# Conditioning rows of a DiT-style block turned into columns by on-chip copies from GpSimd's queue, with six rows' weights read with a stride

## The reference

```python
    silu_c = jax.nn.silu(c)
    silu_cc = jax.nn.silu(c_ctx)[None]
    for l in range(DEPTH):                       # DEPTH = 2
        mod = silu_c @ w_ada[l] + b_ada[l]
        mod_c = silu_cc @ w_ada[l] + b_ada[l]
        sh1, sc1, g1, sh2, sc2, g2 = jnp.split(mod, 6, axis=-1)
        csh1, csc1, cg1, csh2, csc2, cg2 = jnp.split(mod_c, 6, axis=-1)
        h = modulate(rms_norm(x, norm1_g[l]), sh1, sc1)
...
        x = x + g1[:, None, :] * y
        h = modulate(rms_norm(x, norm2_g[l]), sh2, sc2)
        x = x + g2[:, None, :] * expert_choice_ffn(h, ...)
```

## Time and profile before

| | us |
|---|---|
| median of 3 runs | 2315.06 (2312.73 to 2321.35) |
| span of the profiled execution | 2316.9 |
| TensorE busy | 2036.9 (88%) |
| VectorE busy | 670.7 (29%) |
| ScalarE busy | 430.6 (19%) |
| GpSimd busy | 0.2 |
| matmuls of `mod_step`, L1252, 18 pieces | 71.1 |
| turns at L1265, four pieces | 8.3 |
| turns at L1268, eight pieces | 16.4 |
| first block's attentions | about 150 to 270 and 1151 to 1221 |

### The profile page before, as it was taken

The page is one execution under the profiler, slowest core; times in us unless marked ns, Lnnn a source line. Parts: engine busy times, 40 slices in busy tenths (PEclk is TensorE's granted clock), DMA queues, the critical chain, the costliest instruction groups (busy, mean ns, idle before and its releaser), DMA issues.

```text
span 2316.9 us, 21565 instructions
## 1 busy us (share of the span) xinstructions
PE 2036.9 (88%) x8606; PEld 1003.2 (43%) x8606; DVE 670.7 (29%) x1613; ACT 430.6 (19%) x884; POOL 0.2 (0%) x4
## 2 busy tenths in 40 slices
PE   6999899999988889888999978789776688979998
PEld 3445444444432323333554433333222255748863
DVE  2275311124211212124560132122211158730001
ACT  3045300014200000002151022103100032530000
POOL 0000000000000000000000000000000000000000
PEclk8999999999999989998999988999897899989999
DMA  9237722322599999996394548999999963132432
GB/s 366 76 145 304 270 82 64 101 90 109 216 421 422 430 428 429 429 427 243 127 345 137 191 199 330 425 420 422 431 427 429 429 237 109 37 109 102 153 136 82
DMA packets 111614, 598.15 MB, mean 258 GB/s; under 512 B 9255, under 2 KB 15223, under 8 KB 86811
## 3 DMA queue, kind: packets, MB, share of 16 engines
q1 hardware_dynamic: 107920, 591.82, 63.9%
q10 hardware_dynamic: 3595, 4.95, 0.6%
HBM read 595.71 MB, written 1.05 MB: 258 GB/s over the span
## 4 chain that ended last, share of the span: by engine, by line
PE 70%; DMA 21%; DVE 4%; ACT 2%; issue 2%; DVEq 0%; SPq 0%; ACTq 0%
PE bank L1286 24%; DMA weight_ring<-in_w_up_e 14%; PE bank L1696 8%; PE bank L638 7%; PE bank L1723 4%; PE bank L1679 4%; PE bank L657 3%; PE bank L1235 3%; PE bank L1252 3%; DMA weight_ring<-in_w_down_e 2%; DMA arena<-in_w_up_e 2%; PE bank L1522 2%; PE bank L435 2%; PE bank L1456 2%; DMA weight_ring<-in_w_ada 1%
## 5 line engine op out<-in xcount | busy, mean ns | idle before, releaser
L1286 PE MATMUL bank<-weight_ring,arena 128*128 128x512 f32 (+1 forms) x1328 | 562.0, 585 | 4.0 <-DMA weight_ring<-in_w_in 2.0
L1286 PEld LDWEIGHTS bank<-weight_ring,arena 128*128 128x128 f32 x1328 | 252.7, 191 | 308.8 <-issue 299.1
L1696 PE MATMUL bank<-weight_ring,arena 128*64 128x512 f32 x832 | 247.1, 642 | 55.3 <-DMA weight_ring<-in_w_up_e 43.2
L1679 PE MATMUL bank<-weight_ring,arena 128*32 128x512 f32 x816 | 152.5, 767 | 67.4 <-DMA weight_ring<-in_w_up_e 52.7
L1723 PE MATMUL bank<-weight_ring,arena 128*64 128x512 f32 (+1 forms) x800 | 179.1, 593 | 12.3 <-DMA weight_ring<-in_w_down_e 11.2
L1696 PEld LDWEIGHTS bank<-weight_ring,arena 128*64 128x64 f32 x832 | 80.0, 148 | 180.0 <-issue 179.7
L638 PE MATMUL bank<-arena,weight_ring 128*128 128x256 f32 x704 | 153.6, 381 | 0.8 <-DVE small L2339 0.8
L3100 ACT ACTIVATE arena<-bank 64x512 f32<-64x512 f32 (+1 forms) x64 | 37.7, 589 | 624.6 <-PE bank L1696 398.1
L638 PEld LDWEIGHTS bank<-arena,weight_ring 128*128 128x128 f32 x704 | 134.7, 191 | 19.7 <-issue 1.1
L1235 PE MATMUL bank<-const,arena 128*128 128x128 f32 (+3 forms) x764 | 106.1, 286 | 33.8 <-DVE arena L2504 6.4
L1235 PEld LDWEIGHTS bank<-const,arena 128*128 128x128 f32 (+3 forms) x764 | 90.5, 165 | 84.6 <-issue 64.2
(11 more groups left out here) (388 smaller groups left out, 1840.8 us busy)
## 6 DMA issues: line engine op xcount, KB each, us to landing
weight_ring<-in_w_up_e SPq DMA_DIRECT2D x52, 2048.0 KB, 14.3
weight_ring<-in_w_gate_e SPq DMA_DIRECT2D x51, 2048.0 KB, 16.1
weight_ring<-in_w_down_e SPq DMA_DIRECT2D x50, 2048.0 KB, 13.1
weight_ring<-in_w_in SPq DMA_DIRECT2D x25, 2048.0 KB, 10.0
weight_ring<-in_w_ada SPq DMA_DIRECT2D x24, 2048.0 KB, 12.3
arena<-in_w_down_e SPq DMA_DIRECT2D x14, 2048.0 KB, 15.8
arena<-in_w_gate_e SPq DMA_DIRECT2D x13, 2048.0 KB, 16.4
arena<-in_w_up_e SPq DMA_DIRECT2D x12, 2048.0 KB, 17.3
```

The source lines that it names most:

```text
L1286: mm = pe.matmul(b[:, 0:c1 - c0], lhs[:, k, t * P:t * P + P], slot_view(r)[:, k, c0:c1], start=(k == 0), stop=(k == ks - 1))
L1679: mm = pe.matmul(b[c:c + R, :], xgT[1][:, KH * half + k, e, :], wide(r)[:, k, n * 512:n * 512 + 512], start=(half == 0 and k == 0), stop=( ...
L1696: mm = pe.matmul(banks_[n][c:c + R, :], xgT[l][:, KH * half + k, e, 0:R], wide(r)[:, k, n * 512:n * 512 + 512], start=(half == 0 and k == ...
```

## The change

Only `mod_step` inside the attentions changes (`late=True`); the two early pieces are multiplied and turned as before.

- TensorE no longer turns the ten late rows. The matmuls of L1265 are gone altogether, those of L1268 stay for the two early pieces.
- GpSimd gets a stream: for each of the ten rows it waits until the row is in `row_tmp` and issues four DMAs (two streams, two halves of the row), each from one partition to 64 partitions, 8 consecutive numbers for each, into a new tile `mod_turned`.
- VectorE waits on the semaphore of these DMAs (`row_turned0` or `row_turned1`, 64 for four DMAs) in place of a full bank, at the same place, and reads `mod_turned` in place of the bank.
- A copy can only give partition p eight numbers that lie side by side. For the four pieces that want element 8p+k that is right as it is. For the six others, `(1, 0)`, `(1, 1)`, `(2, 0)`, `(2, 1)`, `(2, 3)`, `(2, 4)`, the row itself has to be made in another order: their matmuls at L1252 (L1257 after) read the weights with the inner step of 128 numbers (512 bytes), 8 of them, then the next column. The number of matmuls and of columns stays.

```diff
+        mod_turned = sb("mod_turned", 2, 2, KD)
...
-            def mod_step(cur, turned):
+            def mod_step(cur, turned, late=True):
                 if cur:
                     l, seg = cur
+                    by_partition = late and seg % 3 != 2 and not (l < DEPTH and seg > 2)
...
-                                mm = pe.matmul(b[at:at + 32, :], silu_pad[:, col:col + 32], wide(r)[:, k, n * 512:n * 512 + 512],
+                                row = wide(r)[:, k, n * 512:n * 512 + 512]
+                                if by_partition:
+                                    row = wide(r)[:, k, :].rearrange("q (k p) -> q p k", p=P)[:, 64 * n:64 * n + 64, :]
+                                mm = pe.matmul(b[at:at + 32, :], silu_pad[:, col:col + 32], row,
                                                start=(k == 0), stop=(k == KH - 1))
...
-                if turned:
+                if turned and not late:
                     pe.wait_ge(S("seg_row_ready"), due("seg_row_ready"))
                     pe.wait_ge(S("freeD"), due("freeD"))
                     b = bank_of("D", T.n["freeD"])
...
-                            if turned[0] < DEPTH and turned[1] > 2:
-                                mm = pe.matmul(b[64 * n:64 * n + 64, 2 * k:2 * k + 2], row_tmp[q, k:512:KD], ident[q, pair], start=True, stop=True)
...
+        @block.gpsimd
+        def _(pool):
+            rows_ready = 2
+            for l in range(DEPTH):
+                for _, turned in LATE_STEPS[l].values():
+                    if turned:
+                        rows_ready += 1
+                        at = turned[1] % 3
+                        pool.wait_ge(S("seg_row_ready"), rows_ready)
+                        for n in range(2):
+                            for s in range(2):
+                                q = 64 * at + 32 * n + s
+                                pool.dma_start(mod_turned[64 * n:64 * n + 64, at, s, :],
+                                               row_tmp[q:q + 1, :].rearrange("o (p k) -> o p k", k=KD)).then_inc(S(f"row_turned{at}"), 16)
...
+                    if late:
+                        dve.wait_ge(S(f"row_turned{seg % 3}"), due(f"row_turned{seg % 3}", 4 * 16))
+                        dve.tensor_tensor(col, mod_turned[:, seg % 3, :, :].rearrange("p s k -> p k s"), bias, ALU.add).then_inc(S("dve_step"), 1)
+                        dve.wait_ge(S("dve_step"), due("dve_step"))
```

More of the change, by code:

```diff
@@ L1263, in mod_step @@
                             q, pair = slice(base, base + 34), slice(base + 32 * n, base + 32 * n + 2)
-                            if turned[0] < DEPTH and turned[1] > 2:
-                                mm = pe.matmul(b[64 * n:64 * n + 64, 2 * k:2 * k + 2], row_tmp[q, k:512:KD], ident[q, pair], start=True, stop=True)
-                            elif k // KH == n:
+                            if k // KH == n:
                                 at = (k % KH) * P
@@ L1893, in _ @@
             pe.wait_ge(S("silu_c_ready"), due("silu_c_ready", 2))
-            mod_step(*EARLY_STEPS[0])
+            mod_step(*EARLY_STEPS[0], late=False)
             pe.wait_ge(S("vecs_landed"), 16 * (N_VEC - N_VEC0))
@@ L1899, in _ @@
             mm.then_inc(S("fullD"), 1)
-            mod_step(*EARLY_STEPS[1])
+            mod_step(*EARLY_STEPS[1], late=False)
             turn_half(xn, 0, "A", 1)
             pe.wait_ge(S("silu_c_ready"), due("silu_c_ready", 4))
-            mod_step(*EARLY_STEPS[2])
+            mod_step(*EARLY_STEPS[2], late=False)
             turn_half(xn, 1, "A", 1)
-            mod_step(*EARLY_STEPS[3])
+            mod_step(*EARLY_STEPS[3], late=False)
             pe.wait_ge(S("router_pad_clear"), 1)
@@ L2053, in mod_step @@
                     l, seg = turned
-                    dve.wait_ge(S("fullD"), due("fullD"))
-                    b = bank_of("D", T.n["fullD"])
                     col = mod_cols[:, 2 * l + seg // 3, 1 - seg % 3, :, :]
@@ L2058, in mod_step @@
                     bias = (vec_rows[:, l, seg - 2, :] if by_row else vecs[:, l, 32 + 8 * seg:40 + 8 * seg]).unsqueeze(2).to_broadcast([P, KD, 2])
-                    dve.tensor_tensor(col, b[:, 0:16].rearrange("p (k s) -> p k s", s=2), bias, ALU.add).then_inc(S("freeD"), 1)
-                    dve.wait_ge(S("freeD"), due("freeD"))
+                    if late:
+                        dve.wait_ge(S(f"row_turned{seg % 3}"), due(f"row_turned{seg % 3}", 4 * 16))
+                        dve.tensor_tensor(col, mod_turned[:, seg % 3, :, :].rearrange("p s k -> p k s"), bias, ALU.add).then_inc(S("dve_step"), 1)
+                        dve.wait_ge(S("dve_step"), due("dve_step"))
+                    else:
+                        dve.wait_ge(S("fullD"), due("fullD"))
+                        b = bank_of("D", T.n["fullD"])
+                        dve.tensor_tensor(col, b[:, 0:16].rearrange("p (k s) -> p k s", s=2), bias, ALU.add).then_inc(S("freeD"), 1)
+                        dve.wait_ge(S("freeD"), due("freeD"))
                     if seg % 3 == 1:
@@ L2698, in _ @@
             for step in EARLY_STEPS[1:]:
-                mod_step(*step)
+                mod_step(*step, late=False)
             dve.memset(flag, 0.0).then_inc(S("mod_cols_ready"), 1)
```

## The result

| | before | after |
|---|---|---|
| median of 20 runs, us | 2316.60 | 2323.91 |
| ratio to before, 95% interval | | 1.0034 (1.0023 to 1.0044) |
| span of the profiled execution, us | 2316.9 | 2317.5 |
| layer 0's attention, from piece `(0, 3)` to the router sums | 106.8 | 102.7 |
| layer 1's attention, from piece `(2, 0)` to the router sums | 63.8 | 73.3 |

The change makes the kernel slower by about 7.9 us, 0.34%: a small loss, inside the half per cent that I called no change that can be told, though twenty runs a side do tell it. The two attentions move against each other: layer 0's gets shorter by 4 us, layer 1's longer by 9.5.

The account below looks back on a forecast made before the run. TensorE, busy 88%, bounds the kernel, except where layer 0's attention waits for weights. Removed turns, clock and copies sum to -16.0 us, strided reads +19.9: +3.9 on 2315.1, so 2319 us, range 2296 to 2362.

Parts of the forecast that it names:

- What bounds where: Both attentions: TensorE full in layer 1, a turn costing 1.88 us; in layer 0 weights late from about 214 us.
- the stretch that waits for weights: Layer 0's attention, from the end of piece (1, 0)'s matmuls to (1, 5) at 257.58; removing turns there gains 0.
- Turns removed and the clock: Ten late turns gone: -4.0 and -2.0 us in layer 0, -7.5 in layer 1; clock -3.1; copies +0.7; about -16.
- The 3.1 us for the clock: Layer 0, behind the turns of (0, 3) and (0, 4): TensorE's slowdown goes with them; bounds 0 and 3.1 us.
- Copies: GpSimd's 40 DMAs, 256 packets a row: landing after 8.1 us costs 0; their DMA traffic adds 0.7 us.
- the 2.0 us that the prediction gives beside it: Fixed time for a small DMA issued by GpSimd, from the Trainium skill; the sum would stay as it is.
- Rival 3: Copies land late and VectorE waits in place of TensorE: 17 us at a 13.7 us landing, 2316 us; chance 0.06.
- The stride: Six pieces' matmuls read weights 512 bytes apart; taken as a factor of 2 on the matmuls, price 19.9 us.
- d: Time by which one strided piece becomes longer than a packed one; taken as 3.57 us, bounds 0 and 10.7.
- 6d - 1.5: Price of six longer strided pieces, less 1.5 us that (1, 1) may be late without cost; 19.9 us.
- Rival 1: The strided reads of the six pieces cost nothing: -16.0 us, 2299 us, or 2296.5 with a calmer clock; chance 0.22.
- rival 2: Four strips share the read at L1257, a strided bundle taking up to four times as long: +46.7, 2362 us; chance 0.27.

Follow-up runs that it names:

- experiment 2: Against the changed kernel, all weights read packed, GpSimd still copying all ten rows (six pieces' columns in another order): 2303.59 us, ratio 0.9944 to the kernel before.
- experiment 1: Against the changed kernel, TensorE turns all ten rows again and GpSimd copies nothing; strided weight reads stay: 2345.25 us, ratio 1.0124 to the kernel before.
- experiment 6: Against the changed kernel, a late piece's matmuls reordered so the four column strips run one after another, same output: 2429.68 us in one run.

## Why the prediction was right

Forecast 2319 us, +3.9 us, from a range of 2296 to 2362; measured +7.9 us by the ratio. The mechanism that I took for the likeliest is the one that was there: the turns' gain is taken back by the strided reads. That the time fell inside a range of 66 us says little; the forecast's own, 2312 to 2327, holds it too. Of the 4.9 us between 2319 and 2323.9, 1.5 are the base, three runs against twenty. By its steps:

- **What bounds where.** Held in the main. Turns in the stretch that waits for weights turned into waiting (with the copies alone 10.0 us for 5.3). Those of layer 1 were worth their length in the changed kernel and 4.9 of 7.5 us without the stride. What I left out is that TensorE's clock falls behind these waits, so that longer waits cost something beside the load.
- **Turns removed and the clock**, -16.0 with the copies' cost: measured in experiment 2 as -13.0 (-16.9 to -9.0). Too large in layer 1: I gave the weights of `(2, 5)` 1.6 us to spare, and in experiment 2 TensorE waited 1.79 us for them and 0.70 for VectorE at `(2, 4)`. The four pieces were in 46.6 us after the end of `(2, 0)` there (1194.20 less 1147.62), where I had summed 42.4. The 3.1 us for the clock were seen to be gone in the profile, and both profiles of the kernel before had them; by experiment 1 they are no fixed part of the turn.
- **Copies.** Cost 0 held, VectorE waited 0.3 us. I took the landing as 8.1 us from a row of another queue, and it was 5.1 (4.8 at least, 6.4 at most); the 2.0 us that the prediction gives beside it was not seen either. The packets were half as many as counted. Rival 3 never came near.
- **The stride.** The term that was mis-sized: d = 3.57 us by a factor of 2, measured 4.43 by 2.24. The price 6d - 1.5 becomes 25.1 us, and the sum -16.0 + 25.1 = +9.1, within the measured 5.3 to 10.2. The waits of experiment 2 do not lower it, as with the strided pieces they are not there. The row that led to the factor had about the right size: the strided weight loads of the earlier trace rows, 1.66 against 0.67 ns a column, and not the turns of the earlier trace rows. That the two kinds of read are slow for one reason no run shows, so the size of the factor is in part luck.
- **Rivals.** Rival 1 (free stride) falls by the 8.00 us; rival 2 by experiment 6; rival 3 by the waits.
- **By attention.** Layer 1's was to become longer by 4 x 3.57 - 7.5 = 6.8 us and became 9.5 longer. Its four strided pieces cost 17.9 us more and the turns 7.5 less, and 0.9 of `(2, 0)` is covered: behind it TensorE waited 0.59 us for ScalarE between two groups of turns of the probabilities, and now they run through. I had let all of d through there. Layer 0's was to lose 2.8 (8.4 of gains less 5.7 of stride) and lost 4.1 and 5.7 in the two pairs of profiles. Up to the start of `(1, 0)` it lost 9.0 and 7.7 us, where I had 7.1; from there on it became 4.8 and 2.0 longer, where the sum with d = 4.43 gives 6.1. The rest lies in the spread between profiles, of which the clock behind the waits is a part, and is not assigned.

## What to carry to other kernels

A moving fp32 operand whose neighbours lie 16 bytes or more apart cost TensorE twice its matmul time and a little more (512 columns, 32-wide stationary operand; the turns of the earlier trace rows, 16 in 1.94 us with a stride of 8, did not pay it); put a reordering where an engine with time to spare reads the data anyway, here into VectorE's emptying of the bank, where it cost nothing. Work taken off TensorE is only worth what is on the path in that stretch: 7.5 us of turns gave 4.9 where the weights were near to being late, and nothing clear where they were late already. Small on-chip copies issued by an idle GpSimd are a good way to turn rows into columns when one step of some 9 us lies between making and using them.

## What the runs showed of the hardware that I had not expected

- Two numbers out of each 16 bytes, neighbours or 8 bytes apart, are enough for nearly full pace (3.80 us for a piece read in pairs against 3.64 packed, some 5% more), one is half pace or a little less (7.3 to 8.7 us), with little regard to the step, from 16 to 512 bytes.
- VectorE reads a PSUM bank at a step of 512 bytes as fast as packed: 683 ns for 34x512 in both cases.
- Four column strips side by side are 2.5 times as fast as one after another (3.57 against 8.79 us), not four times.
- Behind waits of 2.8 to 3.7 us for weights a packed piece took 5.0 to 6.6 us in place of 3.64, at a granted clock of 0.54 to 0.72, in both profiles of either kernel and in experiment 2.
